# Modulation columns taken one block earlier, and squares of two feature tiles added on GpSimd before TensorE sums them

## The reference

```python
# first block, layer l (ctx likewise while l == 0)
mx = split(silu(c) @ w_ada[l] + b_ada[l], 6)              # modulation vectors
hx = rmsnorm(x, g_pre_mix) * (1 + mx[1]) + mx[0]
x  = x + mx[2] * rmsnorm(token_mixers(hx, hc, ...), g_post_mix)
hx = rmsnorm(x, g_pre_mlp) * (1 + mx[4]) + mx[3]
x  = x + mx[5] * rmsnorm(square(relu(hx @ w1)) @ w2, g_post_mlp)
# second block, layer l
shift, scale, gate = split(silu(c_2) @ ada_w_2[l] + ada_b_2[l], 3)
h = rms_norm(x, pre_norm) * (1 + scale) + shift           # then three branches, merged into y
x = x + gate * rms_norm(y @ w_out, post_norm)
```

## Time and profile before

| | |
|---|---|
| median of three runs | 3344.05 us (3338.84 to 3344.07) |
| the profiled execution | 3338.16 us, span 3336.4 us |
| PE busy | 3000.8 us, 90% of the span |
| DVE, POOL, ACT busy | 48%, 36%, 32% |
| granted TensorE clock, mean | 0.945 of full speed |
| DMA, mean | 83 GB/s |

### The profile page before, as it was taken

The page is one execution under the profiler, slowest core; times in us unless marked ns, Lnnn a source line. Parts: engine busy times, 40 slices in busy tenths (PEclk is TensorE's granted clock), DMA queues, the critical chain, the costliest instruction groups (busy, mean ns, idle before and its releaser), DMA issues.

```text
span 3336.4 us, 41550 instructions
## 1 busy us (share of the span) xinstructions
PE 3000.8 (90%) x15908; PEld 2412.6 (72%) x15908; DVE 1596.7 (48%) x2851; ACT 1056.0 (32%) x1958; POOL 1187.9 (36%) x862
## 2 busy tenths in 40 slices
PE   7999788898899989968879899999989999999898
PEld 5788677777778867857657676777678767776786
DVE  4673535545555257344533214553482245544822
ACT  3224434121212231344222233233333322333332
POOL 1121142333333422214434452333255623332555
PEclk9999898999999989978989998999999989999999
DMA  5232011323233211103434321212112312221222
GB/s 202 90 138 76 13 55 53 102 101 109 94 114 107 66 57 63 58 23 101 145 106 154 119 89 67 74 64 64 61 60 73 93 64 70 64 70 57 62 75 67
DMA packets 78388, 276.98 MB, mean 83 GB/s; under 512 B 8544, under 2 KB 10848, under 8 KB 77936
## 3 DMA queue, kind: packets, MB, share of 16 engines
q1 hardware_dynamic: 75824, 268.91, 24.3%
q10 hardware_dynamic: 2368, 5.42, 0.4%
HBM read 272.19 MB, written 2.10 MB: 82 GB/s over the span
## 4 chain that ended last, share of the span: by engine, by line
PE 67%; DVE 15%; DMA 6%; ACT 5%; issue 4%; POOL 2%; SPq 0%; DVEq 0%; ACTq 0%; POOLq 0%
PE pb L1104 14%; PE pb L1105 14%; PE pb L1106 14%; DMA RG<-in_W_dram 6%; PE pb L1231 2%; DVE RLT L1861 2%; PE pb L1126 2%; PE pb L1128 2%; PE pb L1127 2%; PE pb L1143 1%; DVE AR L1822 1%; PE pb L1144 1%; PE pb L1145 1%; POOL RGR L2749 1%; PE pb L1189 1%
## 5 line engine op out<-in xcount | busy, mean ns | idle before, releaser
L2749 POOL TENSOR_TENSOR RGR<-RG,WHI 128x512 fp32r<-128x512 f32 x708 | 1002.5, 1426 | 1863.3 <-ACT WHI L2321 1862.3
L2321 ACT ACTIVATE WHI<-RG 128x512 fp32r<-128x512 f32 x708 | 432.5, 623 | 858.9 <-DMA RG<-in_W_dram 434.2
L1104 PE MATMUL pb<-HI,WHI 128*128 128x512 f32 (+1 forms) x880 | 374.8, 426 | 10.5 <-DVE LO L1750 4.9
L1106 PE MATMUL pb<-LO,WHI 128*128 128x512 f32 (+1 forms) x880 | 351.7, 400 | 0.0
L1105 PE MATMUL pb<-HI,RGR 128*128 128x512 f32 (+1 forms) x880 | 351.2, 399 | 0.0
L1104 PE MATMUL pb<-HR,WHI 128*128 128x512 f32 (+1 forms) x768 | 287.3, 374 | 68.0 <-POOL RGR L2749 61.6
L1104 PE MATMUL pb<-HIDR,WHI 128*128 128x512 f32 (+1 forms) x768 | 280.5, 365 | 42.4 <-POOL RGR L2749 17.1
L1106 PE MATMUL pb<-HR,WHI 128*128 128x512 f32 (+1 forms) x768 | 283.7, 369 | 0.0
L1105 PE MATMUL pb<-HR,RGR 128*128 128x512 f32 (+1 forms) x768 | 283.5, 369 | 0.0
L1105 PE MATMUL pb<-HIDR,RGR 128*128 128x512 f32 (+1 forms) x768 | 278.2, 362 | 0.0
L1106 PE MATMUL pb<-HIDR,WHI 128*128 128x512 f32 (+1 forms) x768 | 278.1, 362 | 0.0
(11 more groups left out here) (418 smaller groups left out, 5696.3 us busy)
## 6 DMA issues: line engine op xcount, KB each, us to landing
RG<-in_W_dram SPq DMA_DIRECT2D x504, 512.0 KB, 3.6
XCX<-in_xT_dram ACTq DMA_DIRECT2D x4, 512.0 KB, 11.8
out_dram<-XCX SPq DMA_DIRECT2D x8, 256.0 KB, 2.1
CS<-in_CST_dram ACTq DMA_DIRECT2D x1, 1027.0 KB, 4.8
XCC<-in_ctxT_dram SPq DMA_DIRECT2D x4, 256.0 KB, 13.7
AR<-in_VEC_dram ACTq DMA_DIRECT2D x1, 1024.0 KB, 6.3
CS<-in_CST_dram SPq DMA_DIRECT2D x1, 523.0 KB, 4.3
RG<-in_W_dram SPq DMA_DIRECT2D x2, 256.0 KB, 3.0
```

Source lines behind the costliest of these rows:

```text
L1104: e.matmul(out, hi[:, k, :], xh, start=k == order[0], stop=False)
L1106: i = e.matmul(out, hi[:, k, :], xl, start=False, stop=k == order[7])
L2321: e.activation(WHI[:, u % 2, h * n:h * n + n], RG[:, s % RING, h * n:h * n + n], ACT.Copy).then_inc(*up("weightsA", (u, h)))
L2749: e.tensor_tensor(RGR[:, s % RING, sl], RG[:, s % RING, sl], WHI[:, u % 2, sl].bitcast(F32), SUB).then_inc(*up("weightsG", (u, h)))
```

## The change

`next_column` now takes a loaded column at every call, so a slab asked for at the end of a block is read at the end of the next one. In the norms ACT squares into 4 buffers; after each odd tile a new POOL step `pair` adds the squares of tiles k-1 and k, in place and region by region, and TensorE sums the four added tiles instead of the eight squares. TensorE's wait is on POOL's add; ACT's wait, from the fifth tile on, is on the sums of the pair that used the buffer.

```diff
--- before.py
+++ after.py
@@ -233,7 +233,7 @@
 
     def next_column(self):
 
-        if self.loaded and (len(self.loaded) > 1 or not self.sums):
+        if self.loaded:
             self.step("column", self.loaded.pop(0))
         if self.sums:
             self.column(*self.sums.pop(0))
@@ -956,7 +956,7 @@
 
     def squares_at(tag, i):
         base = 6144 if tag == "x1a" or tag == "x2a" else norms[tag][0]
-        return ar(base + NT * (1 + i % 2), NT)
+        return ar(base + NT * (1 + i % 4), NT)
 
     def first_square(k):
         return ar(norms["x0a"][0] + NT * k, NT)
@@ -1015,7 +1015,6 @@
 
     def tensor(e):
         begun = set()
-        count = {"sq": 0}
         pb7 = {}
 
         def slab(s, nk):
@@ -1222,14 +1221,14 @@
 
         def sum_square(tag, t0, tn, k):
 
-            i = count["sq"]
-            count["sq"] += 1
-            e.wait_ge(*at("normA", ("square", i)))
+            if k % 2 == 0:
+                return
+            e.wait_ge(*at("normG", ("pair", tag, k // 2, t0)))
             first = norms[tag][2][0][0] // 128
             for c in chunks(t0, tn):
-                a = c * 128 - t0
-                m = e.matmul(sum_at(tag, c), squares_at(tag, i)[:, a:a + 128], ones[:, 0:1], start=k == 0 and c == first, stop=k == 7 and c == 5)
-            m.then_inc(*up("normP", ("square", i), ("sums", tag)))
+                m = e.matmul(sum_at(tag, c), squares_at(tag, k - 1)[:, c * 128:c * 128 + 128], ones[:, 0:1], start=k == 1 and c == first,
+                             stop=k == 7 and c == 5)
+            m.then_inc(*up("normP", ("pair", tag, k // 2, t0), ("sums", tag)))
 
         def rstd(tag):
 
@@ -2288,7 +2287,7 @@
                 stages[what[0]](*what[1:])
 
     def scalar(e):
-        count = {"sq": 0, "relu": 0, "rope": None}
+        count = {"relu": 0, "rope": None}
         roped = []
 
         def bank(p, i=0):
@@ -2336,13 +2335,11 @@
             else:
                 e.activation(SPREAD[1], SPREAD[1], ACT.Silu).then_inc(*up("spreadA", 2))
 
-        def square(x, tag):
-
-            i = count["sq"]
-            count["sq"] += 1
-            if i >= 2:
-                e.wait_ge(*at("normP", ("square", i - 2)))
-            e.activation(squares_at(tag, i)[:, 0:x.shape[1]], x, ACT.Square).then_inc(*up("normA", ("square", i)))
+        def square(x, tag, k, t0):
+
+            if k >= 4:
+                e.wait_ge(*at("normP", ("pair", tag, k // 2 - 2, t0)))
+            e.activation(squares_at(tag, k)[:, t0:t0 + x.shape[1]], x, ACT.Square).then_inc(*up("normA", ("square", tag, k, t0)))
 
         def square_out(x, p):
 
@@ -2368,7 +2365,7 @@
             if following[tag]:
                 for t0, tn, _ in norms[tag][2]:
                     e.wait_ge(*at("normG" if k in ON_POOL else "normV", ("x", tag, k, t0)))
-                    square(xc(k, t0, tn), following[tag])
+                    square(xc(k, t0, tn), following[tag], k, t0)
 
         def modSplit(tag, k):
             base, _, regs = norms[tag]
@@ -2749,6 +2746,8 @@
             e.tensor_tensor(RGR[:, s % RING, sl], RG[:, s % RING, sl], WHI[:, u % 2, sl].bitcast(F32), SUB).then_inc(*up("weightsG", (u, h)))
 
         def residual(tag, k):
+            if k % 2 and following[tag]:
+                pair(tag, k)
             if k not in ON_POOL:
                 return
             src = sources[tag][0]
@@ -2757,6 +2756,14 @@
                 x = xc(k, t0, tn)
                 e.wait_ge(*at("normV", ("y", tag, k, t0)))
                 e.tensor_tensor(x, x, src[:, k, t1:t1 + tn], ADD).then_inc(*up("normG", ("x", tag, k, t0)))
+
+        def pair(tag, k):
+
+            new = following[tag]
+            for t0, tn, _ in norms[tag][2]:
+                a, b = [squares_at(new, kk)[:, t0:t0 + tn] for kk in (k - 1, k)]
+                e.wait_ge(*at("normA", ("square", new, k, t0)))
+                e.tensor_tensor(a, a, b, ADD).then_inc(*up("normG", ("pair", new, k // 2, t0)))
 
         def mO(l, c):
             sl = slice(c * 128, c * 128 + 128)
```

## The result

The changed kernel takes 3198.39 us (median of four runs, 3197.63 to 3200.15), the kernel before 3341.45 us (3334.02 to 3344.07); the ratio is 0.9576, with a 95% interval of 0.9559 to 0.9594. The forecast was 3202 us. The profiled execution went from 3338.16 to 3197.63 us, 140.5 us less.

The account below looks back on a forecast made before the run. Bound: a loop of waits between column reads and weight slab transfers in the MLPs. From 3338.16 us, minus 136 (columns) and 3.5 (norms), 3198.7; half of 5.9 us added for the median: 3202 us, 8 in 10 within 3186 to 3228.

Parts of the forecast that it names:

- The loop and its excess, 146 us: MLP blocks beside columns: a loop of waits through DVE, SP, slab and ACT costs 75 us in layer 0, 71 in layer 1.
- 12.20 / 2 and 9.95 / 2 us a turn, under the block: Both MLPs: the loop spans two blocks, 6.10 and 4.98 us a block, under 8.42 and 5.59, so it stops binding.
- (a): Weight slab's own slot: in layer 1 the second half's split is ready after some 6 us, needed at 8.4; fits.
- (b): Column's own slab, read one block sooner by DVE: 14 us to spare in layer 0, 7 in layer 1; no wait.
- (c): Change from `relu2` to `plus`: 8 us of PE's waits stay, plus 2 us for clock dips, leaving 136 of 146 us.
- ACT's wait for DMA under 30 us: Sign of success: ACT's 247.6 us of waiting before weight slabs that have not landed falls under 30 us.
- The norms, 3.5 us of gain: Five norms: half of TensorE's sums go, POOL adds come; gain 1.3 us with two regions, 0.3 with one, 3.5 in all.
- Rival B: Columns gain as forecast, but the SBUF port shared by DVE and POOL makes the norms 17.5 us slower: 3222 us; chance 0.10.
- The sum: Whole kernel: 3338.16 - 136 - 3.5 = 3198.7 us in the profiled execution's terms, 3202 us as the forecast.
- A: Weight ring: the slab's own slot binds with three slabs, only half of the 146 us is won, about 3268 us; chance 0.10.
- C: Both MLPs, 84 columns: DVE waits for unlanded column slabs, evacuations stand behind, nothing won, 1 us lost each: 3428; chance 0.02.
- D: Blocks beside columns: DVE and POOL getting in each other's way sets PE's time, not transfers; near 3340 us; chance 0.02.

Follow-up runs that it names:

- late release: Kernel with the columns' edit alone, but SP loads into the column's slot only at the old kernel's moment, DVE still reading at the new place: 3347.19 us, ratio 1.0011.

## Why the prediction was right, and where it was not

- **The loop and its excess, 146 us.** Right. From root to root around the two MLPs the time fell from 632.5 to 559.55 and from 442.01 to 369.73 us, 145.2 us. The late release, which closed the loop again, gave all of it back. The count behind the 146 was less exact than it looked: before, DVE's column line in layer 0 has 23 steps of 11.3 to 13.4 us, not some 20 of 12.20, and wins part of that back at 4.3 us each time `plus` begins. That 20 turns of 3.78 us gave the same 76 us as the window was in part luck.
- **12.20 / 2 and 9.95 / 2 us a turn, under the block.** Right: blocks at 8.42 and 5.59 us, and a shorter member of the loop gives nothing once it is open.
- **What is late next.** (a) and (b) fit: no wait of DVE for a column, none of PE for a split. (c) was too careful: the 10 us left for the passage from `relu2` to `plus` and for clock dips were not needed. Those waits, too, were the loop's: before, at the longest of them, the last evacuation stood behind ACT's split, and that behind the slab. The term measured 145, not 136. The kernel before, in order of time:

```profile
1621.26 0.63 ACT L2321 ACTIVATE WHI<-RG 128x512 fp32r<-128x512 f32 x1 [6.28 <-DMA RG<-in_W_dram]
1621.80 0.58 ACT L2483 ACTIVATE RLT<-pb 128x512 f32<-128x512 f32 x1
...
1625.28 0.79 PE L1104 MATMUL pb<-HIDR,WHI 128*128 128x512 f32 x1 [5.41 <-DVE HIDR L1863]
```

- **ACT's wait for DMA under 30 us.** Right in layer 0, of which it was said: 247.6 us before, no such wait after. In layer 1, for which the prediction gave no figure, 75.1 of 176.9 us stay: the slab is still not there when ACT comes to its split, but TensorE doesn't wait for what follows.
- **The norms, 3.5 us of gain.** Wrong in sign, and longer norms stood among its own signs of being wrong: 4.3 us of loss from root to root (3.1 to 3.5 in the pairs of executions with the same columns). Three prices failed. The chain over POOL was put at 3.8 us a pair and measured 4.2, since POOL's update stands until DVE's is through (1.71 us and not 1.27), so the last of POOL's adds ended at 1873.6 (13.4 us behind the first, not 12.7); from there to the root it was 2.4 us and not 1.9. In the two-region norm DVE ended 3.0 us later, not 2, and the root came 23.7 us after DVE's first instruction, where 20.6 to 22.4 was said. The sums did halve, to 192 records from 384. Rival B had the mechanism, with 17.5 us a price four times too high, as it charged every pair add the longest POOL time seen.
- **The sum.** 3198.7 us was said for the profiled execution, 3197.63 came: 9 us too little in the columns and 8 too much in the norms cancelled. A good total hid a wrong term; only the root to root times showed it.
- **Rivals A, C and D.** A's part of the loop did not stay. C: no wait of DVE for a slab. D fell with the late release, which has DVE's new order and the old time.

## What to carry to other kernels

When a transfer queue is served in strict order and slots are freed by an engine that is itself fed, one step back, by what the queue brings, look for the loop: follow the chain of waits until the same instruction comes again, and compare the length of one turn with the length of one block. What opens it is to span one block more (here by reading the slot's guest sooner), and then the length of one member no longer mattered (3202 us with the shorter one, 3200 without). An operation given to an idle engine isn't free. See what stands behind it in that engine's queue, and put it behind the last thing that others wait for. Price it with its neighbour's wait for the port.

## What the runs showed of the hardware

A short DVE instruction with two SBUF inputs takes as long as POOL's lets it: 128 elements took 1.26 us beside a POOL split of 2.3 us, and 0.29 at the least, by the line's own spread:

```profile
L1659 DVE SCALAR_TENSOR_TENSOR RG<-RG,AR x48: 291/1253/1266, 589.4 to 1035.1; 128x128 f32<-128x128 f32 x48
```

The lock of which the Trainium skill speaks (SBUF — State Buffer, Who interferes with whom) is seen here from both sides: DVE stands behind POOL (1.67 against 0.69 us), and POOL behind DVE (1.71 against 1.27: POOL's update starts at 1863.97, while DVE's runs from 1863.36 to 1864.56).

The granted clock behind a norm differs between executions of the same kernel (0.83 or 1.00 over 20 us), worth 3.1 us in 3200: differences of that size are to be read off stretches, not off the whole.
